# Three edits to a mixer-and-experts kernel: another order in the projection, another order of cells and mixers, and h2 computed in routing from x1

## The chip, the core and the metric

The kernel runs on one core of a Trainium2 chip. The core has TensorE (PE) for matmuls, VectorE (DVE), ScalarE (ACT) and GpSimd (POOL) for the rest, and SyncE (SP), which only issues transfers. The metric is the device time of one launch in microseconds (us); lower is better.

## The reference

One layer of a backbone for 1152 tokens of 1024 channels, all float32: 128 context tokens and 1024 latent ones.

```
h  = modulate(rmsnorm(x));  z = h @ w_in                      # 2832 columns
x  = x + gate1 * ([mLSTM(z) || windowed attention(z)] @ w_out)
h2 = modulate(rmsnorm(x, n2), sh2, sc2)
x  = x + gate2 * peer(h2)
def peer(h, ...):             # P_HEADS 8, P_DKEY 256, P_TOPK 16, N_KEYS 128
    q = h @ w_q                                       # 2048 columns
    sa, sb = q-halves against sub_a, sub_b            # 2 x 128 scores a head
    va, ia = top_k(sa, 16);  vb, ib = top_k(sb, 16)
    top, pos = top_k(va + vb, 16)                     # of 256 sums
    eidx = (ia * 128 + ib)[pos];  gates = softmax(top)
    a = gelu(h . u_tab[eidx]);  return sum((gates * a) * v_tab[eidx])
```

Each token picks 128 experts (8 heads, 16 each), and each expert is a row of u and a row of v, 8 KB together. The mLSTM runs over the tokens forward and backward; latent tokens start from cached states.

## The kernel before

The tokens are nine tiles of 128; tile 0 holds the context. Three stages follow one another.

*Conditioning* turns the conditioning vectors into shifts, scales and gates.

*Projection* (`project_in`, lines 280 to 560). A loop over the tiles, one body for each engine. TensorE turns the tile's normalised x (eight 128x128 blocks, `in_xn` to the PSUM banks `in_xT0` and `in_xT1`); VectorE and ScalarE copy the turned halves, scaled and shifted, to `in_hT`; TensorE multiplies by six column blocks of w_in (five of 512 columns, one of 272; b counts them), and other engines copy each block out, norm the attention heads, rotate them, and store all to DRAM. At the end of a tile q and k are turned, through the same two banks, and then the heads and the gates. `in_hT` exists once.

*Mixing and experts* (`mix_and_experts`). Four generators write each engine's program: `mlstm()` does 18 cell units of three steps each (two directions for each of nine tiles); `mixer(t)` does attention, w_out and x1 = x + gate1 * mix of a tile in 19 sub-steps and stores x1, h2 and h2 turned (h2T) to DRAM; `route(t)` loads h2T and does queries, scores, the top-16s and the expert numbers of a tile in 45 steps; `pair(t, r)` is the work on one pair of gathers. A tile's experts are 128 gathers in 64 pairs: a gather (line 992, GpSimd) brings one expert row for each of 128 partitions, 1.05 MB, into one of eight buffers `fx_ring`. Each of a pair's gathers serves 64 tokens with two slots each, so h2 lies in a buffer `fx_h2` with its 64 rows twice, and is loaded by four transfers of 64 partitions a tile. VectorE takes the dot product with h2 (line 1647), ScalarE the gelu and its weight, and TensorE adds the weighted v rows up (line 1239); then the buffer is free and GpSimd may issue the gather for the pair four further on. `route(t+1)` must have ended before the first gather of tile t+1.

The order is fixed by `drive`, the same on all engines. Ahead of the first gather (the lead) stand the cells, the mixer and the route of tile 0; the rest is interleaved with the pairs (the stream):

```
for _ in range(LEAD): next(cells)                                      # LEAD 4
for _ in range(SUBS): next(cells, None); next(subs)                    # SUBS 19
for _ in range(STEPS): next(cells, None); next(steps, None)            # STEPS 45
...
for r in range(PAIRS):
    pair(t, r)
    if t or r >= LAG: next(steps, None)                                # LAG 19
    if due(t, r): next(subs, None)
def due(t, r):
    return t == 0 and r < LAG or (t < 2 and r % 4 != 3) or t == 2
```

w_q is streamed in chunks of 0.52 MB, sixteen a tile, for the first `STREAMED` = 4 tiles, and then stays in SBUF as `rt_w_q`. SyncE issues the loads in program order: at the start of mixing the cached keys and values, masks, x, w_out, subT and wq, and behind them the cells' (`load_cell`). y of tile t-1 is stored in pair 12 of tile t.

## Time and profile before

| | before |
|---|---|
| median of 3 runs | 4085.48 us (4083.76 to 4090.05) |
| the profiled execution | 4090.53 us, of which the span 4088.7 us |
| mean granted clock of TensorE | 0.822 |
| PE, DVE, ACT, POOL busy | 69%, 58%, 24%, 35% of the span |
| gathers: share of 16 DMA engines' span | 72.2% |
| first and last gather issued | 915.8 us, 4065.4 us |

The busy shares are means over stages with different limits: ahead of the first gather the DMA queues are nearly empty, and behind it they are nearly full. Times in the trace count from the span's start. The projection's matmuls run from 119.68 to 576.21 us.

### The profile page before, as it was taken

To read this page: it belongs to the slowest core of one execution; us is meant where nothing else is said; L and a number is where in the kernel's file an instruction comes from. 1 tells how busy PE (TensorE), PEld (TensorE's weight loads), DVE (VectorE), ACT (ScalarE), POOL (GpSimd) and SP (SyncE) were. 2 spreads that over 40 slices of the span, in tenths; PEclk is the share of its full clock that TensorE was granted. 3 is DMA by queue.
4 is the path that set the end of the run, shared out by engine and by line. 5 is a ranking of instruction groups with operands and counts; after the bars stand their busy time and mean duration, and the time that the engine had idled before them with its cause. 6 is when DMAs were issued, how large, how long until landed. Compare 5 with 4: busy or idle time off the path is not lost.

```text
span 4088.7 us, 30827 instructions
## 1 busy us (share of the span) xinstructions
...
## 2 busy tenths in 40 slices
...
GB/s 411 54 42 42 42 116 94 169 120 404 401 404 351 416 405 384 420 420 404 371 420 405 411 421 406 421 409 403 421 407 403 421 410 421 405 401 421 421 422 371
DMA packets 228539, 1399.54 MB, mean 342 GB/s; under 512 B 25890, under 2 KB 36770, under 8 KB 75810
## 3 DMA queue, kind: packets, MB, share of 16 engines
q0 software_dynamic: 165888, 1208.03, 72.2%
q1 hardware_dynamic: 54724, 166.11, 11.0%
...
## 4 chain that ended last, share of the span: by engine, by line
DMA 43%; PE 19%; DVE 12%; issue 4%; POOL 4%; ACT 3%; SPq 0%; ACTq 0%; POOLq 0%; DVEq 0%
DMA fx_ring<-arg_uv,fx_eidx 40%; PE fx_acc L1239 10%; DVE fx_ring L1647 6%; POOL fx_ring L992 4%; PE at_sP L1107 2%; ACT fx_weighted_pick L1375 2%; DMA rt_wq<-arg_w_q 1%; PE rt_qP L1137 1%; DVE rt_rest L1527 1%; DVE rt_ab L1529 1%; DVE rt_rest L1525 1%; PE at_aP L1071 1%; DMA ml_v<-kv_scratch 1%; PE at_sP L1137 1%; ACT fx_gelu L1371 1%
## 5 line engine op out<-in xcount | busy, mean ns | idle before, releaser
L1239 PE MATMUL fx_acc<-fx_ring,fx_weighted_pick 128*64 128x512 f32 x4608 | 1495.1, 783 | 1046.6 <-ACT fx_weighted_pick L1375 1019.3
L1647 DVE CUSTOM_DVE_ANT_0 fx_ring<-fx_ring,fx_h 128x1024 f32<-128x1024 f32 x1152 | 1406.3, 1228 | 978.7 <-DMA fx_ring<-arg_uv,fx_eidx 973.7
L992 POOL DMA_INDIRECT fx_ring<-arg_uv,fx_eidx x1152 | 1318.3, 1144 | 1834.5 <-PE fx_acc L1239 1599.8
L1239 PEld LDWEIGHTS fx_acc<-fx_ring,fx_weighted_pick 128*64 128x64 f32 x4608 | 338.6, 164 | 2079.0 <-ACT fx_weighted_pick L1375 1488.8
L1371 ACT ACTIVATE fx_gelu<-fx_dot 128x2 f32<-128x2 f32 x576 | 117.1, 203 | 2287.1 <-DVE fx_dot L1647 2268.4
L411 PE MATMUL in_z<-w_in,in_hT 128*128 128x512 f32 (+1 forms) x864 | 365.7, 587 | 34.6 <-DVE in_hT L500 29.4
L1375 ACT ACTIVATE fx_weighted_pick<-fx_weighted_pick,fx_gelu 128x64 f32<-128x64 f32 x1152 | 338.1, 340 | 54.5 <-ACT fx_gelu L1371 1.5
L411 PEld LDWEIGHTS in_z<-w_in,in_hT 128*128 128x128 f32 x864 | 171.4, 200 | 224.9 <-issue 217.2
L1137 PE MATMUL rt_qP<-rt_w_q,rt_h2T 128*128 128x512 f32 x320 | 162.2, 630 | 0.0
L379 POOL COPY in_turned<-in_heads 128x320 f32<-128x320 f32 x9 | 4.1, 452 | 411.6 <-DVE in_heads L521 411.6
L1107 PE MATMUL at_sP<-at_w_out,at_mixT 128*128 128x512 f32 x288 | 133.8, 607 | 0.0
L1137 PE MATMUL rt_qP<-rt_wq,rt_h2T 128*128 128x512 f32 x192 | 106.5, 681 | 28.9 <-DMA rt_wq<-arg_w_q 22.3
L1018 POOL TENSOR_TENSOR ml_k<-ml_k,ml_cols 128x512 f32<-128x512 f32 x18 | 19.0, 1055 | 254.6 <-ACT ml_cols L1343 177.7
L249 DVE SCALAR_TENSOR_TENSOR gate_softplus<-gate_forget,gate_softplus 64x128 f32<-64x128 f32 x9 | 2.5, 283 | 178.4 <-ACT gate_softplus L242 178.4
L1639 DVE TENSOR_TENSOR fx_weighted_pick<-fx_pick,fx_gates 128x512 f32<-128x512 f32 x144 | 101.2, 703 | 2.1
L1647 DVE DVE_READ_ACCUMULATOR2_ANT fx_dot<- 128x1 f32 x1152 | 95.0, 82 | 0.0
L1137 PEld LDWEIGHTS rt_qP<-rt_w_q,rt_h2T 128*128 128x128 f32 x320 | 56.1, 196 | 113.8 <-issue 113.8
L1393 DVE CUSTOM_DVE_ANT_0 at_s<-at_sP,at_mask,at_sink_negated 128x512 f32<-128x512 f32 x72 | 52.5, 749 | 52.3 <-PE at_sP L1055 47.9
L1107 PEld LDWEIGHTS at_sP<-at_w_out,at_mixT 128*128 128x128 f32 x288 | 53.5, 194 | 77.3 <-issue 77.3
L1071 PE MATMUL at_aP<-att_v,at_pT 128*128 128x64 f32 x432 | 65.8, 293 | 0.0
L169 PE MATMUL ada_acc<-ada_w,ada_silu 128*2 128x512 f32 x192 | 41.2, 952 | 32.8 <-DMA ada_w<-arg_w_ada 32.8
L1055 PE MATMUL at_sP<-att_kT,at_qT 64*128 64x384 f32 x144 | 62.2, 514 | 0.0
(272 smaller groups left out, 2492.4 us busy)
## 6 DMA issues: line engine op xcount, KB each, us to landing
...
fx_ring<-arg_uv,fx_eidx POOLq DMA_INDIRECT x1152
...
fx_h<-h_scratch SPq DMA_DIRECT2D x36, 256.0 KB, 11.0
...
```

Source lines behind the costliest of these rows:

```text
L411: mm = pe.matmul(zp[b % 3][:, 0:n], hT[:, k, :], g.w_in[:, k, c0:c0 + n], start=(k == 0), stop=(k == KD - 1))
L992: pool.indirect_dma_start(out=ring[j][:], out_offset=None, in_=io.uv, in_offset=bass.IndirectOffsetOnAxis(ap=eidx[t % 2][:, i:i + 1], axis=0),
L1055: pe.matmul(ST[h % 2][:, P:4 * P], lhs, g.akT[half, t * P:t * P + 3 * P], start=True, stop=True).then_inc(s_sc, 1)
L1071: mm = pe.matmul(aP[:, h * ADH:(h + 1) * ADH], pT[h % 2][:, j * P:(j + 1) * P], rhs, start=(j == 0), stop=(j == 3))
L1107: mm = pe.matmul(ST[half][:], mixT[:, j, :], w_out[:, j, half * 512:(half + 1) * 512], start=(j == 0), stop=(j == KD - 1))
L1137: mm = pe.matmul(qq[b][:], hq2T[:, k, :], w[:, b * 512:(b + 1) * 512], start=(k == 0), stop=(k == KD - 1))
L1239: mm = pe.matmul(acc[b][cg * TOKS:(cg + 1) * TOKS, :], wsel[:, i % (2 * FILL), :], ring[i % GROUP][:, D + b * 512:D + (b + 1) * 512], star ...
L1371: act.activation(gelu[:, sl], dot[:, sl], ACT.Gelu_apprx_tanh).then_inc(s_gelu, 1)
L1375: last = act.activation(wsel[:, i, :], wsel[:, i, :], ACT.Copy, scale=gelu[:, i:i + 1])
L1393: dve.tensor_tensor_reduce(out=s[h % 2][:], in0=ST[h % 2][:], in1=mask[:], scale=-float(ADH) ** -0.5, scalar=nsink[:, h:h + 1], op0=ALU.ad ...
L1639: dve.tensor_tensor(wsel[:, lo:lo + FILL, :], pick[:].unsqueeze(1).to_broadcast([P, FILL, TOKS]), gates[t % 2][:, r * NC:r * NC + FILL].un ...
L1647: dve.tensor_tensor_reduce(out=ring[j][:, 0:D], in0=ring[j][:, 0:D], in1=h2r[t % 2][cg][:], scale=1.0, scalar=0.0, op0=ALU.mult, op1=ALU.a ...
```

## The change

1. *Projection.* `in_hT` exists twice. The turn of the next tile's x stands behind this tile's block 2 (`turn_x`), that of q behind block 4, and q and k are turned through a bank of their own, `in_qkTp`. ScalarE and VectorE scale the next tile's halves in between, GpSimd norms a tile ahead, and the loops are unrolled by two.
2. *Order in mixing.* The loads of the first two cells go to the head of SyncE's queue. Six cell steps stand ahead of the mixer (before: four), one beside every second sub-step of the mixer and of the first routing steps. A mixer has 15 sub-steps and a route 49. In the stream mixers take one sub-step in every pair of tiles 0 and 1; the route of tile 1 begins at pair 15 and takes five steps in four pairs. w_q is streamed for three tiles.
3. *h2 and h2T.* They are no longer stored or loaded. `route(t)` loads x1 (into the lower half of `rt_scores`, `x1r`), norms and turns it (k = 1 to 4), and at k = 28 and 29 makes the doubled rows of h2 with TensorE (`rows`), whose two halves VectorE and ScalarE copy to `fx_h2`.

```diff
-        hT = sb("in_hT", [P, KD, P])
+        hT = [sb(f"in_hT{i}", [P, KD, P]) for i in range(2)]
...
+        qkTp = psum("in_qkTp")
...
+                def turn_x(t):
                     pe.wait_ge(s_xn, t + 1)
-                    if not first:
-                        pe.wait_ge(s_qkTe, t * 2)
                     for k in range(KD):
                         mm = pe.transpose(xTp[k // 4][:, (k % 4) * P:(k % 4 + 1) * P], xn[:, k * P:(k + 1) * P], g.ident[:])
                     mm.then_inc(s_xT, 1)
+
+                def turn_head(t, i):
+                    pe.wait_ge(s_za, t * 4 + (i + 1))
+                    for h in range(MH):
+                        src = q[:, h * P:(h + 1) * P] if i == 0 else kv[:, h * P:(h + 1) * P]
+                        mm = pe.transpose(qkTp[:, h * P:(h + 1) * P], src, g.ident[:])
+                    mm.then_inc(s_qkT, 1)
+
+                def tile(t, par, first=False, last=False):
...
-                            mm = pe.matmul(zp[b % 3][:, 0:n], hT[:, k, :], g.w_in[:, k, c0:c0 + n],
+                            mm = pe.matmul(zp[b % 3][:, 0:n], hT[par][:, k, :], g.w_in[:, k, c0:c0 + n],
                                            start=(k == 0), stop=(k == KD - 1))
                         mm.then_inc(s_z, 1)
-                    for i in range(2):
-                        pe.wait_ge(s_za, t * 4 + (i + 1))
-                        for h in range(MH):
-                            src = q[:, h * P:(h + 1) * P] if i == 0 else kv[:, h * P:(h + 1) * P]
-                            mm = pe.transpose(xTp[i][:, h * P:(h + 1) * P], src, g.ident[:])
-                        mm.then_inc(s_qkT, 1)
+                        if b == 2 and not last:
+                            turn_x(t + 1)
+                        if b == 4:
+                            if not first:
+                                pe.wait_ge(s_qkTe, t * 2)
+                            turn_head(t, 0)
+                    pe.wait_ge(s_qkTe, t * 2 + 1)
+                    turn_head(t, 1)
...
+                    if not last:
+                        scaled(t + 1, 1 - par, 1)
...
-    SUBS = 19
+    SUBS = 15
...
-    LEAD = 4
+    LEAD = 6
     NG = NSIDE // 4
-    STEPS = 45
+    TURN = 4
+    ROWS = TURN + 24
+    STEPS = TURN + 45
     WQ = 2
-    STREAMED = 4
-    LAG = 19
+    STREAMED = 3
+    LAG = SUBS
...
     def due(t, r):
-        return t == 0 and r < LAG or (t < 2 and r % 4 != 3) or t == 2
+        return t < 2
 
     def drive(begin, pair, mixer, route, mlstm):
 
@@ -587,12 +628,14 @@
         for _ in range(LEAD):
             next(cells)
         subs = chain.from_iterable(mixer(t) for t in range(TILES))
-        for _ in range(SUBS):
-            next(cells, None)
+        for k in range(SUBS):
+            if k % 2:
+                next(cells)
             next(subs)
         steps = route(0)
-        for _ in range(STEPS):
-            next(cells, None)
+        for k in range(STEPS):
+            if k % 2 or k > 10:
                 next(cells, None)
...
                 if t or r >= LAG:
                     next(steps, None)
+                    if t == 0 and r % 4 == 3:
+                        next(steps, None)
...
+        x1r = sc[:, 0:NSIDE // 2, :].rearrange("p s k -> p (s k)")
...
-                        if k == 17:
-                            sp.wait_ge(s_hTe, t * 2 + 2)
-                            sp.dma_start(g.h2T_dram[t], h2T[:].rearrange("p k n -> p (k n)")).then_inc(s_hTo, 16)
-                            if t + 1 < TILES:
-                                sp.wait_ge(s_x1o, t * 16 + 16)
-                                sp.wait_ge(s_xn, t + 1)
-                                sp.dma_start(x1[:], io.x[t + 1]).then_inc(s_x, 16)
-                        if k == 18:
-                            sp.wait_ge(s_h2a, t + 1)
-                            sp.wait_ge(s_h2d, t + 1)
-                            sp.dma_start(g.h2_dram[t], h2[:]).then_inc(s_h2o, 16)
...
-                    if t:
-                        sp.wait_ge(s_qd, t * NSIDE)
-                    sp.wait_ge(s_hTo, t * 16 + 16)
-                    sp.dma_start(hq2T[:].rearrange("p k n -> p (k n)"), g.h2T_dram[t]).then_inc(s_hT, 16)
-                    for k in range(NSIDE):
-                        chunk(t * NSIDE + k + WQ)
-                        yield
-
-                def load_h2(t):
-                    sp.wait_ge(s_h2o, t * 16 + 16)
-                    if t >= 2:
-                        sp.wait_ge(s_dot, (t - 1) * SLOTS)
-                        sp.wait_ge(s_st, (t - 1) * 16)
-                    for cg in range(NC):
-                        for half in range(NC):
-                            sp.dma_start(h2r[t % 2][cg][half * TOKS:(half + 1) * TOKS, :],
-                                         g.h2_dram[t, cg * TOKS:(cg + 1) * TOKS, :]).then_inc(s_h[t % 2], 16)
+                    for k in range(STEPS):
+                        if k == 0 and t:
+                            sp.wait_ge(s_route, t)
+                            sp.wait_ge(s_x1o, t * 16 + 16)
+                            sp.dma_start(x1r, g.x1_dram[t]).then_inc(s_xr, 16)
+                        half, j = divmod(k - TURN, 11)
+                        if 0 <= half < 2 and j < KD:
+                            chunk(t * NSIDE + half * KD + j + WQ)
+                        yield
...
                 def begin():
-                    sp.wait_ge(s_hd, UNITS)
                     for d in range(2):
                         sp.wait_ge(s_hst[d], 16 * TILES)
-                    load_h2(0)
...
-                    if t == STREAMED - 2 and r == PAIRS - 12:
+                    if t == STREAMED - 2 and r == PAIRS - 4:
...
+                load_cell(0)
+                load_cell(1)
                 for cg in range(AKV):
...
+                    def turn_x1():
+                        pe.wait_ge(s_xn, t + 1)
+                        if t:
+                            pe.wait_ge(s_h2a, t * NC)
+                            pe.wait_ge(s_h2d, t * NC)
+                        for j in range(KD):
+                            mm = pe.transpose(qq[j // 4][:, (j % 4) * P:(j % 4 + 1) * P], qs[:, j * P:(j + 1) * P], g.ident[:])
+                        mm.then_inc(s_xT, 1)
+
+                    def rows(cg):
+                        pe.wait_ge(s_qT, t * NG + NG)
+                        if cg:
+                            pe.wait_ge(s_h2a, t * NC + cg)
+                            pe.wait_ge(s_h2d, t * NC + cg)
+                        for j in range(KD):
+                            for half in range(NC):
+                                mm = pe.matmul(qq[j // 4][half * TOKS:(half + 1) * TOKS, (j % 4) * P:(j % 4 + 1) * P],
+                                               hq2T[:, j, cg * TOKS:(cg + 1) * TOKS], g.ident[:], start=True, stop=True)
+                        mm.then_inc(s_h2p, 1)
+
                     for k in range(STEPS):
-                        half, j = divmod(k, 11)
-                        if half < 2:
+                        if k == 3:
+                            turn_x1()
+                        half, j = divmod(k - TURN, 11)
+                        if 0 <= half < 2:
                             if j < KD:
                                 query(half, j)
                             if j == 8:
@@ -1164,6 +1199,8 @@
                                 score(2 * half)
                             if j == 10:
                                 score(2 * half + 1)
+                        if ROWS <= k < ROWS + NC:
+                            rows(k - ROWS)
...
+                        if k == 1:
+                            if t:
+                                act.wait_ge(s_xr, t * 16)
+                            else:
+                                act.wait_ge(s_x1, 2)
+                            act.activation(qs, x1t, ACT.Square, accum_out=ss[:]).then_inc(s_sq, 1)
+                        if k == 2:
+                            act.wait_ge(s_ms, t + 1)
+                            act.activation(ss[:], ss[:], ACT.Sqrt).then_inc(s_rt, 1)
+                        if k == 3:
+                            act.wait_ge(s_rr, t + 1)
+                            act.activation(qs, x1t, ACT.Copy, scale=ss[:]).then_inc(s_xn, 1)
+                        if k == 4:
+                            act.wait_ge(s_xT, t + 1)
+                            cnd = min(t, 1)
+                            for j in range(4, KD):
+                                last = act.activation(hq2T[:, j, :], qq[1][:, (j - 4) * P:(j - 3) * P], ACT.Identity,
+                                                      bias=g.shift[:, 1, j, cnd:cnd + 1], scale=g.scale[:, 1, j, cnd:cnd + 1])
+                            last.then_inc(s_hTe, 1)
+                        if ROWS < k <= ROWS + NC:
+                            cg = k - ROWS - 1
+                            act.wait_ge(s_h2p, t * NC + cg + 1)
+                            if t >= 2:
+                                act.wait_ge(s_st, (t - 1) * 16)
+                            act.activation(h2r[t % 2][cg][:, 512:D], qq[1][:], ACT.Copy).then_inc(s_h2a, 1)
...
+                        if ROWS < k <= ROWS + NC:
+                            cg = k - ROWS - 1
+                            dve.wait_ge(s_h2p, t * NC + cg + 1)
+                            if t >= 2:
+                                dve.wait_ge(s_st, (t - 1) * 16)
+                            dve.tensor_copy(h2r[t % 2][cg][:, 0:512], qq[0][:]).then_inc(s_h2d, 1)
```

On TensorE's queue a tile of the projection stood like this (tile 0 before; `in_z` is a block's product, `in_xT` the turned x, and then q and kv):

```order
L395 MATMUL in_xT<-ident,in_xn 128x128 x8
L411 MATMUL in_z<-w_in,in_hT 128x512 x8
L411 MATMUL in_z<-w_in,in_hT 128x272 x8
L411 MATMUL in_z<-w_in,in_hT 128x512 x32
L418 MATMUL in_xT<-ident,in_q 128x128 x4
L418 MATMUL in_xT<-ident,in_kv 128x128 x4
L425 MATMUL in_aqTp<-ident,in_heads 128x128 x4
L426 MATMUL in_akTp<-ident,in_heads 128x128
L427 MATMUL in_akTp<-ident,in_gates 128x128
```

and now (tile 1 of the kernel after):

```order
L432 MATMUL in_z<-w_in,in_hT 128x512 x8
L432 MATMUL in_z<-w_in,in_hT 128x272 x8
L432 MATMUL in_z<-w_in,in_hT 128x512 x8
L408 MATMUL in_xT<-ident,in_xn 128x128 x8
L432 MATMUL in_z<-w_in,in_hT 128x512 x16
L415 MATMUL in_qkTp<-ident,in_q 128x128 x4
L432 MATMUL in_z<-w_in,in_hT 128x512 x8
L415 MATMUL in_qkTp<-ident,in_kv 128x128 x4
L448 MATMUL in_aqTp<-ident,in_heads 128x128 x4
L449 MATMUL in_akTp<-ident,in_heads 128x128
L450 MATMUL in_akTp<-ident,in_gates 128x128
```

The turn of x stands behind the third block and is the next tile's; that of q stands ahead of the last block.

On VectorE's queue, the last steps of the lead, the expert numbers of tile 0 (`rt_rest`, `rt_ab`) and the gates, before:

```order
L1527 TENSOR_TENSOR rt_rest<-rt_rest,rt_val 128x1024
L1529 TENSOR_REDUCE rt_ab<-rt_rest 128x64
L1525 TENSOR_TENSOR rt_rest<-rt_pos_partf,rt_iota 128x1024
L1527 TENSOR_TENSOR rt_rest<-rt_rest,rt_val 128x1024
L1529 TENSOR_REDUCE rt_ab<-rt_rest 128x64
L1525 TENSOR_TENSOR rt_rest<-rt_pos_partf,rt_iota 128x1024
L1527 TENSOR_TENSOR rt_rest<-rt_rest,rt_val 128x1024
L1529 TENSOR_REDUCE rt_ab<-rt_rest 128x64
L1535 SCALAR_TENSOR_TENSOR fx_eidx<-rt_ab 64x64 x4
L1538 TENSOR_REDUCE rt_gsum<-rt_gexp 128x8
L1539 RECIPROCAL rt_gsum<-rt_gsum 128x8
L1545 TENSOR_TENSOR fx_gates<-rt_gexp,rt_gsum 64x64 x4
```

and now, from the second of the four one-hot groups on, with cells (`ml_` names) between them:

```order
L1575 TENSOR_TENSOR rt_rest<-rt_pos_partf,rt_iota 128x1024
L1577 TENSOR_TENSOR rt_rest<-rt_rest,rt_val 128x1024
L1579 TENSOR_REDUCE rt_ab<-rt_rest 128x64
L1619 TENSOR_TENSOR ml_e<-fx_acc,ml_e 128x512
L1575 TENSOR_TENSOR rt_rest<-rt_pos_partf,rt_iota 128x1024
L1577 TENSOR_TENSOR rt_rest<-rt_rest,rt_val 128x1024
L1579 TENSOR_REDUCE rt_ab<-rt_rest 128x64
L1629 SCALAR_TENSOR_TENSOR ml_c<-ml_c,ml_cols,rt_qP 128x129 x2
L1634 TENSOR_TENSOR ml_num<-ml_num,fx_acc 128x258
L1629 SCALAR_TENSOR_TENSOR ml_c<-ml_c,ml_cols,rt_qP 128x129 x2
L1634 TENSOR_TENSOR ml_num<-ml_num,fx_acc 128x258
L1636 SCALAR_TENSOR_TENSOR ml_den<-ml_num 128x4
```

The last cell unit has moved from ahead of all of these rows into them.

On SyncE's queue, a late tile of the stream before (h2T for the next route, x1 and y of the tile before, h2 for the next tile):

```order
L863 DMA rt_h2T<-h2T_scratch 128x1024
L881 DMA fx_h_1_0<-x_scratch 128x1024
L885 DMA result_y<-fx_h_1_0 128x1024
L875 DMA fx_h_1_0<-h_scratch 64x1024 x2
L875 DMA fx_h_1_1<-h_scratch 64x1024 x2
L863 DMA rt_h2T<-h2T_scratch 128x1024
```

and now, two tiles (x1 for the next route, x1 and y of the tile before):

```order
L899 DMA rt_scores<-x_scratch 128x1024
L908 DMA fx_h_0_0<-x_scratch 128x1024
L912 DMA result_y<-fx_h_0_0 128x1024
L899 DMA rt_scores<-x_scratch 128x1024
L908 DMA fx_h_1_0<-x_scratch 128x1024
L912 DMA result_y<-fx_h_1_0 128x1024
```

The four loads of 64 partitions and that of h2T are gone, and one of x1 has come.

## Rows read from the trace of the kernel before

**Rows 1.** The page, DMA queues: packets, MB, share of 16 engines.

```profile
q0 software_dynamic: 165888, 1208.03, 72.2%
```

**Rows 2.** Line 992: count, issue ns (low, median, maximum), first to last start.

```profile
L992 POOL DMA_INDIRECT fx_ring<-arg_uv,fx_eidx x1152: 935/941/3041, 915.8 to 4065.4; - x192
```

**Rows 3.** Stretches: length; PE, PEld, DVE, ACT, POOL busy; PEclk, DMA share, GB/s.

```profile
3800.00:4000.00 200.00, 114.35 (x320) 24.96 (x318) 105.34 (x172) 31.58 (x120) 85.33 (x80) 0.75 1.01 422
2473.00:2805.00 332.00, 206.86 (x626) 54.60 (x628) 223.15 (x496) 59.16 (x208) 146.35 (x128) 0.81 1.01 413
1415.00:1789.00 374.00, 289.16 (x1096) 118.96 (x1096) 260.24 (x587) 132.34 (x324) 167.63 (x139) 0.89 1.00 406
1280.00:1320.00 40.00, 25.61 (x73) 8.00 (x73) 32.18 (x50) 6.28 (x19) 10.83 (x10) 0.82 0.61 245
2480.00:2500.00 20.00, 10.46 (x36) 3.85 (x35) 8.40 (x24) 3.17 (x11) 7.36 (x6) 0.83 1.02 341
850.00:915.00 65.00, 23.88 (x158) 20.26 (x156) 59.21 (x195) 9.68 (x36) 3.61 (x5) 0.70 0.28 85
```

**Rows 4.** GpSimd's timeline at the end of tile 0: start, length, row.

```profile
1306.79 0.94 POOL L992 DMA_INDIRECT fx_ring<-arg_uv,fx_eidx  x1 [20.60 <-PE fx_acc L1239]
```

**Rows 5.** Stretches of the projection, columns as in rows 3.

```profile
366.10:419.20 53.10, 44.79 (x119) 22.40 (x118) 15.20 (x34) 13.01 (x20) 2.70 (x3) 0.87 0.11 41
378.00:384.00 6.00, 5.92 (x7) 2.50 (x8) 0.00 (x0) 0.30 (x1) 0.00 (x0) 0.50 0.00 0
```

**Rows 6.** TensorE's timeline in the projection.

```profile
119.68 40.79 PE L411 MATMUL in_z<-w_in,in_hT 128*128 128x512 f32 x96 [1.69 <-ACT in_hT L440]
...
372.12 1.97 PE L395 MATMUL in_xT<-ident,in_xn 128*128 128x128 f32 x8 [4.32 <-ACT in_qkT L464]
378.08 41.31 PE L411 MATMUL in_z<-w_in,in_hT 128*128 128x512 f32 x96 [3.99 <-DVE in_hT L500]
...
576.21 0.60 PE L418 MATMUL in_xT<-ident,in_q 128*128 128x128 f32 x4
```

**Rows 7.** ScalarE's timeline in the projection.

```profile
412.56 0.60 ACT L453 ACTIVATE in_kv<-in_z 128x512 f32<-128x512 f32 x1 [6.27 <-PE in_z L411]
```

**Rows 8.** VectorE's timeline, the last cell step.

```profile
879.60 0.69 DVE L1591 TENSOR_TENSOR ml_h<-ml_num,ml_den 128x512 f32<-128x512 f32 x1
```

**Rows 9.** SyncE's queue at the start of mixing.

```profile
586.94 1.20 SPq L945 DMA_DIRECT2D at_cache_kT<-arg_cache_kT  x2
...
718.89 0.33 SPq L835 DMA_DIRECT2D x_scratch<-at_x  x1
```

**Rows 10.** VectorE's timeline at the start of mixing.

```profile
608.10 0.17 DVE L1658 TENSOR_SCALAR at_sink_negated<-at_sink 128x8 f32<-128x8 f32 x1 [20.83 <-DMA rt_subT<-arg_subT]
...
616.98 0.69 DVE L1569 TENSOR_TENSOR ml_e<-fx_acc,ml_e 128x512 f32<-128x512 f32 x1 [8.71 <-PE fx_acc L1209]
```

**Rows 11.** TensorE's timeline, the first query.

```profile
744.59 1.98 PE L1137 MATMUL at_sP<-rt_wq,rt_h2T 128*128 128x512 f32 x4 [2.05 <-DMA rt_h2T<-h2T_scratch]
```

**Rows 12.** VectorE by line, 600 to 877 us: busy, mean ns, idle before.

```profile
L1579 DVE SCALAR_TENSOR_TENSOR ml_c<-ml_c,ml_cols,rt_qP 128x129 f32<-128x129 f32 x68 | 20.5, 344 | 13.7 <-PE rt_qP L1218 13.6
L1584 DVE TENSOR_TENSOR ml_num<-ml_num,fx_acc 128x258 f32<-128x258 f32 x34 | 14.2, 417 | 1.0 <-PE fx_acc L1225 1.0
L1569 DVE TENSOR_TENSOR ml_e<-fx_acc,ml_e 128x512 f32<-128x512 f32 x18 | 12.5, 692 | 82.2 <-PE fx_acc L1209 76.1 <-issue 6.0
L1591 DVE TENSOR_TENSOR ml_h<-ml_num,ml_den 128x512 f32<-128x512 f32 x17 | 12.3, 725 | 0.6
```

**Rows 13.** VectorE by line, 2473 to 2805 us.

```profile
L1647 DVE CUSTOM_DVE_ANT_0 fx_ring<-fx_ring,fx_h 128x1024 f32<-128x1024 f32 x128 | 156.2, 1225 | 107.8 <-DMA fx_ring<-arg_uv,fx_eidx 107.1
L1639 DVE TENSOR_TENSOR fx_weighted_pick<-fx_pick,fx_gates 128x512 f32<-128x512 f32 x16 | 11.0, 690 | 0.3
L1647 DVE DVE_READ_ACCUMULATOR2_ANT fx_dot<- 128x1 f32 x128 | 10.6, 83 | 0.0
L1527 DVE TENSOR_TENSOR rt_rest<-rt_rest,rt_val 128x1024 f32<-128x1024 f32 x4 | 4.9, 1226 | 0.1
```

252 lines of the change are left out of this document (120 added, 132 removed).

## The prediction

> **What bounds the kernel now.** I read the page's queues first: the gathers of expert rows move 1208 MB [rows 1]. The first is issued at 915.8 us, the last at 4065.4 us [rows 2], so the kernel is a lead of 916 us and a stream of 4088.7 - 915.8 = 3173 us. Then the table of stretches. Where nothing runs beside the gathers, DMA is at a share of 1.01 and 422 GB/s, and VectorE is busy for half the time [rows 3]; 1208/422 = 2863 us, and the stream's other 310 us are other bytes and dips. Two kinds of dip stand in [rows 3]: 245 GB/s at a share of 0.61 for 40 us at the end of tile 0, and 341 GB/s *at a share of 1.02*, where the queues are full but slow. The first is a real gap: GpSimd, which issues the gathers, sat 20.60 us [rows 4]. The row names TensorE's last release, but the next gathers also need the route of the next tile, whose 45 steps begin at pair 19 and end exactly with pair 63. The stretches 1415 to 1789 and 2473 to 2805 are tiles from one store of y to the next, one with a mixer and one without: 374 and 332 us [rows 3], against 134.2/0.422 = 318 us for a tile's gathers alone.
>
> In the lead TensorE is the bound. A tile of the projection lasts 53.1 us and gives VectorE 15.20 and ScalarE 13.01 us of work [rows 5]. TensorE waits 4.32 us for a copy out of xT, turns xn, waits 3.99 us for hT, and needs 41.31 us for the six blocks [rows 6]; ScalarE sees a full block every 6.27 + 0.60 = 6.87 us [rows 7]. Behind the wait the granted clock is 0.50, the 1.2 GHz level [rows 5]. At the lead's end, from the last cell step at 879.6 us [rows 8], VectorE works alone until the first gather.
>
> **The change, part by part. Projection.** turn_x of the next tile moves behind block 2 of this one, hT gets a second buffer, q and k turn into a bank of their own. Five full blocks and the narrow one of 272 columns (6.87 x 272/512 = 3.65) are 38.0 us; eight turns of xn 1.0 (1.97 us at 1.2 GHz [rows 6], half of it at 2.4 GHz), q and k 1.0 for the same eight turns, heads and gates 0.6: 40.6 us a tile. The old waits are hidden by the blocks behind block 2 (some 20 us, against the 8.3 us of both waits). MATMULs now run from 119.68 to 576.21 us, 456.5 us [rows 6]. New: the first tile 41.31 + 1.5, as it still starts cold, and eight of 40.6, 367.6. **-89 us**; bounds -71 (the low clock returns at each seam, 41.31 - 38.0 = 3.3 us a tile, for part of the eight: 18 us) and -95. The work on the gates that stood behind the last tile now runs inside it, so the 10.7 us from 576.21 to the next stage's first issue at 586.94 [rows 6, 9] shrink by about 4: **-4**.
>
> **Cell loads.** They go ahead of 14 other loads. But VectorE's first operation waits for subT, the load behind w_out (608.10 [rows 10]), which now has the cells' bytes ahead of it. The first cell's VectorE step, 616.98 [rows 10], moves to about 611: -6 us, part of the walk below.
>
> **Lead-in steps.** Counted from the stage's start at 586.9, before: x1 stored at 132, first query 157.7 [rows 9, 11], gates 328 (first gather less 0.9). A cell unit, three steps, costs VectorE 20.5 + 14.2 + 12.5 + 12.3 us over 17 units, 3.5, with its small steps 4.0 [rows 12]. TensorE's share of one is 23.88/4 = 6.0 us, as four units fill its work between 850 and 915 [rows 3]; so a unit costs 4.0 to 10 us, a step 3.3 at most. Ahead of x1 stood 4 + 17 cell steps, now 6 + 7: eight fewer, 26 us. x1 comes at 132 - 6 - 26 = 100 if the mixer's own chain allows it and at 126 if it does not; I take 113. From there the norm, the turn and hT are five hops between engines; before they had a store and a load of h2T among them and took 25.7 us [rows 9, 11], I take 13: query at 126. From the query to 850 us, where the last scores are made (263 on this count), it took 105 us with 23 cell steps; now it is 19: 92, scores at 218. Now the bill for the cells put off: 20 steps stand behind the scores and not 8, four units more. The old remainder is the 65 us from 850 to 915, 59.21 of them VectorE's and 23.88 TensorE's [rows 3]. So 218 + 65 + 16 to 40. TensorE has 41 free us there, so I take 20 near the low end, and 3 for the copies of h2: 306. **-22 us**; bounds -1 and -40 (x1 at 100 and full overlap). The new row matmuls, 32 of 128 columns, lie between cell steps that wait for VectorE: nothing here, 8 us without that cover (four times 1.97 [rows 6]).
>
> **Stream, bytes.** One x1-sized tensor is 0.524 MB. Gone: h2 and h2T stores of 8 tiles 8.4 MB, h2T loads 4.2, h2 loads (both halves twice) 8.4, 16 chunks of w_q, as tile 3 reads the resident copy, 8.4. Added: 8 loads of x1, 4.2. Net -25.2 MB at 422 GB/s, **-60 us**. It counts in full because the share is 1.0 with a mixer or without [rows 3].
>
> **Stream, the slow load.** The dip to 341 GB/s is where the four h2 loads of 64 partitions run: (422 - 341) x 20 us = 1.6 MB, 3.8 us beyond their own bytes, eight times **-31 us** [rows 3]. The Trainium skill (SBUF — State Buffer, "Door 1: The DMA port swizzle") says that 64 partitions reach only half of the 16 ports, some 218 GB/s; by that the 1.05 MB would cost 4.8 instead of 2.5 us, eight times 18 us in all. The trace agrees in kind, and the sum goes by the row.
>
> **Stream, dips.** The route of tile 1 now takes five steps in four pairs from pair 15 and ends near pair 53, so the gap of [rows 4] goes: 40 us x (422 - 245)/422 = 17 us saved. Against it, mixers run a sub-step in *every* pair of tiles 0 and 1. Of VectorE's 223.15 us in a tile without a mixer, 156.2 + 10.6 + 11.0 are the gathers' dots and picks [rows 3, 13], 2.8 us a pair; the other 45 us are routing and y, in 34 of 64 pairs 1.3 us each. Mixer steps cost (260.24 - 223.15)/51 = 0.7, in the 51 of that stretch's pairs that have one. Together 4.8 us, against 5.9 us that a pair of tile 0 takes. Where a one-hot step runs (3 x 1.22 [rows 13]), a pair needs 7.2, for four pairs. I add 9 us in tile 0, 16 in tile 1 (16 more pairs with a mixer, and 8 us of new seams) and take off 8 in tile 2, free of mixers. Net 0; bounds -15 and +40. The norm chain in routing adds about 7 us of VectorE and ScalarE a tile in steps of up to 2 us, shorter than the eight buffers' lead. The x1 load for route(1) waits for a store only one step old, and ScalarE's Square behind it, with four pairs of gathers in flight. SyncE's wait on s_route ahead of x1r holds back nothing, as the old tile's y and x1 are issued by then.
>
> **Sum.** -89 - 4 - 22 - 60 - 31 + 0 = -206 us against the profiled execution's 4090.5 us, 3884; that one lies 5 us above the median of 4085.5, so 3879, of which I name 3878 us.
>
> **Rivals.**
> *A. The bytes were hidden (the stream is bound by the ring's round trip).* For it: GpSimd waits for TensorE's release of a buffer before a gather [rows 4]. Against: 422 GB/s at full share in the last tile. Then only lead and slow load gain: 3878 + 60 = 3938. 8 in 100.
> *B. Crowded tiles 0 and 1 cost more.* If each of the 120 pairs with a mixer step misses its time by 0.5 us: 3938 too. For it: 32.18 us of VectorE in the 40 us of 245 GB/s [rows 3]. 12 in 100. **The slower end:** the same place, if VectorE and TensorE run in turn: 260.24 + 289.16 = 549 us for a tile that takes 374 [rows 3], 175 more, two tiles 350: 4228. It decides from 104 us a tile on (207/2), 1.6 us a pair. Against: both overlap today. 2 in 100. The Trainium skill (SBUF — State Buffer, "Who interferes with whom") says that VectorE can block GpSimd's descriptor writing through their shared port; the trace shows a gather's issue at 0.941 us as median and 3.041 at most [rows 2], two of the latter a pair would be this case's mechanism.
> *C. The projection is not freed* (the chain of ScalarE's copies and table loads becomes its bound at 46 us a tile; only 13.01 us of work speak against): +43, 3921. 8 in 100.
> *D. More overlap:* lead -40, dips -15: 3845. 15 in 100.
> *E. Forecast as summed,* 55 in 100.
>
> **How the numbers follow.** The predicted time is E's. D and E's low side end near 3840; A, B and C lie at 3921 to 3938. The range 3838 to 3925 leaves out A, B and the slower end, 2 in 10. A difference of 0.2%, 8 us, is about what a measurement of this kernel can tell from none. All cases but the slower end are faster: 0.97, 0.01, 0.02.
>
> **What would show it.** Projection: MATMULs of one tile 40 to 41 us apart, clock 1.0, their end near 487. First gather near 800 us; VectorE's last ml_h within 7 us of the gates. No 341 GB/s at full share anywhere. No 20 us wait of GpSimd at tile 0's end, but dips near pairs 45 to 53. Period of late tiles 325 to 328 us. Wrong if the share falls below 0.9 for long in tiles 0 and 1, or if a tile of the projection takes over 44 us.

## The result and the profile after

The changed kernel took 3929.9 us (median of 4, 3924.5 to 3942.4) against 4086.6 us before; the ratio is 0.962 (95% interval 0.9596 to 0.9645). The prediction was 3878 us, with 3838 to 3925 as its range: the sign was right, the gain of 157 us was 52 us short, and the time lies outside the range. All times are medians of undisturbed runs: one run of `extra_late` of 9031 us, at a granted clock of 0.525, is left out.

Where the gain came from follows from four points of the trace. In the projection a tile lasts 40.4 us (before 53.1 [rows 5]), as TensorE's timeline shows between two turns of x:

```profile
380.92 1.04 PE L408 MATMUL in_xT<-ident,in_xn 128*128 128x128 f32 x8
381.80 13.90 PE L432 MATMUL in_z<-w_in,in_hT 128*128 128x512 f32 x32
...
421.33 1.04 PE L408 MATMUL in_xT<-ident,in_xn 128*128 128x128 f32 x8
```

421.33 - 380.92 = 40.4 us, no wait is noted, and the turn of eight blocks takes 1.04 us and not 1.97 [rows 6]. The last turn of kv stands at 482.8 us. SyncE's first issue of the next stage comes at 489.65, and the first gather at 804.7:

```profile
489.65 0.34 SPq L925 DMA_DIRECT2D ml_qkT<-qkT_scratch  x1
...
L1011 POOL DMA_INDIRECT fx_ring<-arg_uv,fx_eidx x1152: 935/941/3054, 804.7 to 3906.7; - x192
```

(SyncE's queue; then line 1011 as in [rows 2].) So the first gather comes 111 us earlier, where the working of the prediction has 115. The rest of the kernel is the stream: 3930.6 - 804.7 = 3125.9 us against 3172.9, 47 us less, where 91 were forecast. **44 of the 48 us that the profiled execution is off are in the stream.** Between stores of y its tiles took (us from the first gather or the last store):

| | to y of tile 0 | tile 1 | tile 2 | tiles 3 to 7, each |
|---|---|---|---|---|
| before | 499.1 | 373.8 | 352.6 | 331.6 to 333.2 |
| after | **516.8** | 367.5 | 325.2 | 326.1 to 327.2 |

The table of stretches says the same, with columns as in [rows 3]. To y of tile 0 before:

```profile
915.80:1415.00 499.20, 380.35 (x1454) 161.22 (x1455) 310.74 (x712) 177.76 (x423) 209.03 (x180) 0.87 0.97 392
```

After, to y of tile 0, then of tile 1, then a late tile:

```profile
804.70:1321.50 516.80, 422.90 (x1682) 195.28 (x1684) 314.68 (x707) 194.54 (x448) 214.09 (x180) 0.87 0.93 366
1321.50:1689.00 367.50, 287.85 (x1146) 122.14 (x1144) 248.52 (x568) 126.50 (x311) 158.55 (x132) 0.85 0.98 395
2340.70:2666.80 326.10, 209.01 (x698) 60.35 (x696) 225.72 (x503) 66.60 (x219) 144.71 (x128) 0.83 1.01 416
```

Late tiles run at full DMA share, 6.1 us shorter than before (the means of the five are 332.6 and 326.4 us). Tile 0 is longer than before although it moves fewer bytes, 366 GB/s x 516.8 us = 189 MB against 392 x 499.2 = 196; its share is 0.93 and was 0.97. GpSimd's 20.6 us wait of [rows 4] is gone. Before, it stood beside two others of over 9 us (10.95 and 9.25); now there are seven of 8.7 to 14.3 us up to y of tile 0. Two of them, with GpSimd's first columns as in [rows 4]:

```profile
917.54 1.19 POOL L1011 DMA_INDIRECT fx_ring<-arg_uv,fx_eidx  x1 [14.30 <-PE fx_acc L1276]
...
947.97 1.74 POOL L1011 DMA_INDIRECT fx_ring<-arg_uv,fx_eidx  x1 [12.23 <-PE fx_acc L1276]
```

**The first** has its cause on ScalarE's and SyncE's timelines. SyncE issued the load of x1 for routing at 903.07, and ScalarE, whose Square needs it, stood until it had landed, 8.5 us later; the gelus of the gathers waited behind. SyncE's queue, then ScalarE:

```profile
903.07 0.33 SPq L899 DMA_DIRECT2D rt_scores<-x_scratch  x1
...
898.20 0.59 ACT L1416 ACTIVATE fx_weighted_pick<-fx_weighted_pick,fx_gelu 128x64 f32<-128x64 f32 x2
911.60 1.06 ACT L1321 ACTIVATE rt_scores<-rt_scores 128x1024 f32<-128x1024 f32 x1 [12.82 <-DMA rt_scores<-x_scratch]
```

**The second** is a chain through all engines. The timeline of all engines, 932 to 949 us (rows of other work are left out):

```profile
932.76 0.20 ACT L1412 ACTIVATE fx_gelu<-fx_dot 128x2 f32<-128x2 f32 x1 [0.67 <-DVE fx_dot L1698]
933.06 0.59 ACT L1416 ACTIVATE fx_weighted_pick<-fx_weighted_pick,fx_gelu 128x64 f32<-128x64 f32 x2
933.20 1.98 PE L1151 MATMUL rt_qP<-rt_wq,rt_h2T 128*128 128x512 f32 x4
...
938.53 3.64 PE L1151 MATMUL rt_qP<-rt_wq,rt_h2T 128*128 128x512 f32 x4 [3.34 <-DMA rt_wq<-arg_w_q]
...
944.99 0.75 DVE L1434 CUSTOM_DVE_ANT_0 at_s<-at_sP,at_mask,at_sink_negated 128x512 f32<-128x512 f32 x1 [12.27 <-PE at_sP L1074]
...
945.75 1.94 PE L1276 MATMUL fx_acc<-fx_ring,fx_weighted_pick 128*64 128x512 f32 x8
945.79 0.72 ACT L1295 ACTIVATE at_s<-at_s,at_negmax 128x512 f32<-128x512 f32 x1 [10.84 <-DVE at_negmax L1434]
```

A pair's weights are ready at 933.65. Its accumulation (L1276) starts at 945.75, 12.1 us later, because two query steps stand ahead of it on TensorE's queue (an extra step), the second waits 3.34 us for its chunk of w_q and then runs at 3.64 us in place of 1.98 (the granted clock from 938.5 to 942.2 us is 0.54), and the mixer's matmuls follow. VectorE, ScalarE and GpSimd all wait for that one queue, and none of them was short of time.

### The profile page after: what moved, and what is told of

It reads as the page before. It is cut to its first block, busy times and chain, and to the rows that moved or that the text cites. A ratio compares the mean times of both kernels' runs of the same rounds, so it can differ in the third digit from the quotient of the medians.

```text
span 3930.6 us, 31619 instructions
## 1 busy us (share of the span) xinstructions
PE 2791.8 (71%) x10020; PEld 1090.0 (28%) x10020; DVE 2367.0 (60%) x5341; ACT 952.1 (24%) x2673; POOL 1419.3 (36%) x1269
## 4 chain that ended last, share of the span: by engine, by line
DMA 39%; PE 22%; DVE 13%; ACT 4%; issue 4%; POOL 4%; SPq 0%; ACTq 0%; POOLq 0%; DVEq 0%
DMA fx_ring<-arg_uv,fx_eidx 37%; PE fx_acc L1276 11%; DVE fx_ring L1698 7%; POOL fx_ring L1011 4%; PE at_sP L1128 3%; ACT fx_weighted_pick L1416 2%; DMA rt_wq<-arg_w_q 2%; PE at_aP L1090 1%; PE rt_qP L1151 1%; DVE rt_rest L1577 1%; DVE rt_ab L1579 1%; DVE rt_rest L1575 1%; PE at_sP L1074 1%; PE at_sP L1151 1%; ACT fx_gelu L1412 1%
## 5 line engine op out<-in xcount | busy, mean ns | idle before, releaser
L1276 PE MATMUL fx_acc<-fx_ring,fx_weighted_pick 128*64 128x512 f32 x4608 | 1471.5, 772 | 986.8 <-ACT fx_weighted_pick L1416 962.5
L1276 PEld LDWEIGHTS fx_acc<-fx_ring,fx_weighted_pick 128*64 128x64 f32 x4608 | 333.6, 161 | 1999.4 <-ACT fx_weighted_pick L1416 1446.7
L432 PE MATMUL in_z<-w_in,in_hT 128*128 128x512 f32 (+1 forms) x864 | 348.1, 561 | 1.7 <-DVE in_hT L533 1.7
L432 PEld LDWEIGHTS in_z<-w_in,in_hT 128*128 128x128 f32 x864 | 162.8, 191 | 168.5 <-issue 160.8
L1151 PE MATMUL rt_qP<-rt_w_q,rt_h2T 128*128 128x512 f32 x384 | 194.2, 629 | 0.0
L1151 PEld LDWEIGHTS rt_qP<-rt_w_q,rt_h2T 128*128 128x128 f32 x384 | 66.8, 194 | 132.5 <-issue 132.5
L1698 DVE DVE_READ_ACCUMULATOR2_ANT fx_dot<- 128x1 f32 x1152 | 94.9, 82 | 0.0
L1151 PE MATMUL rt_qP<-rt_wq,rt_h2T 128*128 128x512 f32 x128 | 68.1, 659 | 14.4 <-DMA rt_wq<-arg_w_q 14.3
L1484 DVE TENSOR_TENSOR at_xn<-at_sP,at_gate 128x512 f32<-128x512 f32 x18 | 12.4, 691 | 97.5 <-PE at_sP L1128 97.5
```

Of the source, the lines that this page charges most:

```text
L432: mm = pe.matmul(zp[b % 3][:, 0:n], hT[par][:, k, :], g.w_in[:, k, c0:c0 + n], start=(k == 0), stop=(k == KD - 1))
L1151: mm = pe.matmul(qq[b][:], hq2T[:, k, :], w[:, b * 512:(b + 1) * 512], start=(k == 0), stop=(k == KD - 1))
L1276: mm = pe.matmul(acc[b][cg * TOKS:(cg + 1) * TOKS, :], wsel[:, i % (2 * FILL), :], ring[i % GROUP][:, D + b * 512:D + (b + 1) * 512], star ...
L1698: dve.tensor_tensor_reduce(out=ring[j][:, 0:D], in0=ring[j][:, 0:D], in1=h2r[t % 2][cg][:], scale=1.0, scalar=0.0, op0=ALU.mult, op1=ALU.a ...
```

## The experiments

All are variants of the changed kernel, except `p_only`. "Edit" shows what differs. To see where a kernel loses its time in tile 0, I read the issue times of the gathers off GpSimd's timeline. The figures are us between pairs, so 12 pairs at the gathers' own rate are 60 us:

| pairs | 0-14 | 14-26 | 26-44 | 44-60 | 60-64 | 0-64 |
|---|---|---|---|---|---|---|
| before | 71.6 | 70.7 | 113.9 | 94.1 | 40.6 | 391.0 |
| after | 69.6 | 85.8 | 140.5 | 99.6 | 21.9 | 417.3 |
| after_again | 68.4 | 84.9 | 132.6 | 104.7 | 21.9 | 412.4 |
| late_norm | 70.4 | 76.1 | 135.6 | 101.1 | 22.7 | 405.8 |
| extra_early | 71.3 | 84.4 | 130.4 | 95.5 | 24.3 | 405.9 |
| extra_late | 69.1 | 77.7 | 115.2 | 105.4 | 24.8 | 392.1 |
| no_extra | 68.3 | 76.8 | 115.0 | 93.1 | 41.8 | 394.9 |
| late_noextra | 72.2 | 65.3 | 110.2 | 96.5 | 48.3 | 392.5 |
| best1 | 69.4 | 65.3 | 113.3 | 94.9 | 30.5 | 373.3 |
| best2 | 111.6 | 75.0 | 106.2 | 94.3 | 32.2 | 419.1 |
| no_chunks | 71.5 | 81.2 | 116.7 | 99.6 | 23.4 | 392.4 |

### The projection alone

The kernel before with `project_in` of the changed one.

> The kernel before with the changed projection alone. The trace of the changed kernel has a projection tile every 40.4 us and MATMULs from 120 to 483 us (before: to 576 us), so if the projection's gain reaches the end undiminished the time is 4086.6 - 93 - 4 = 3990 us. If it were partly given back behind it (cell loads or tables that were hidden before), 4000 us or more.

3990.2 us (ratio 0.9758, 0.9742 to 0.9775), 95 us less than before. The projection's gain arrives whole.

### The extra routing steps and the norm chain

```diff
 no_extra:
-                    if t == 0 and r % 4 == 3:
-                        next(steps, None)
 late_norm (Square at k == 3, and all of the chain two later):
-    TURN = 4
+    TURN = 6
-                        if k == 1:
+                        if k == 3:
```

> The changed kernel without the extra routing step in tile 0 (one step a pair from pair 15, 49 steps, so the route of tile 1 ends exactly with pair 63 again). Theory 1 (tile 0 is crowded: a mixer step in every pair and five routing steps in four pairs queue behind each other on TensorE and ScalarE): less crowding in pairs 15 to 53, but the wait for the route at the end of tile 0 comes back, 15 to 20 us; sum 3920 to 3935 us. Rival (the loss is one stall of ScalarE for the x1 load, crowding costs nothing): the wait alone comes back, 3930 + 17 = 3947 us.

> The changed kernel with the norm, turn and copies of x1 two routing steps later (the Square at step 3, the load of x1 still at step 0), so that a load that is 8.5 us under way has three pairs, 18 us, to land. In the changed kernel ScalarE stood 12.8 us for that load in tile 0 and GpSimd 14.3 us behind it. Theory 2 (this stall is lost time for the ring): 10 to 14 us less, 3918 us. Theory 1 alone (the ring would have been late anyhow): 3928 to 3932 us.

no_extra took 3894.6 us (0.9539, 0.9523 to 0.9555): 35 us *less*, below all that either theory gave, although GpSimd stood 21.85 us for the route at tile 0's end again. late_norm took 3919.3 us (0.9588, 0.9572 to 0.9604), 10.6 less. That is no more than the spread of this kernel (see after_again below), so the pairs 14 to 26 of the table must carry the reading: there the stall is 9 to 10 us between the changed kernel and late_norm, and 11.5 us between no_extra's 76.8 and late_noextra's 65.3. The load's stall was lost time. late_norm did not remove it whole: beside the extra step of pair 15 the Square still came early, ScalarE stood 5.41 us for the load, and GpSimd 13.93 us behind it. In best1, which has no extra step there, ScalarE's wait is 1.81 us, and in late_noextra there is none.

### Which extra steps

```diff
 extra_early:
-                    if t == 0 and r % 4 == 3:
+                    if t == 0 and r % 4 == 3 and r < 36:
 extra_late:
+                    if t == 0 and r % 4 == 3 and r >= 36:
```

> The changed kernel with the extra routing steps of tile 0 only at pairs 15 to 35 (six of thirteen, all while routing does its queries and scores on TensorE with streamed chunks of w_q). Without any extra step the kernel took 3894.6 us, 35 us less than with thirteen, although a wait of 21.9 us for the route stood at tile 0's end again. Theory T (the extra steps cost where they put two query steps, their chunks and a mixer step behind one pair on TensorE): nearly all of the loss is here, 3920 to 3930 us. Theory V (they cost where VectorE's top-16 and one-hot steps pile up): none of it is here, and the route ends at pair 57, so 3880 to 3890 us.

> The changed kernel with the extra routing steps of tile 0 only at pairs 39 to 63 (seven of thirteen, behind the queries and scores). Theory T: the loss of the early steps and the wait for the route at tile 0's end are both gone, 3875 to 3888 us. Theory V: the loss is here, 3915 to 3930 us.

extra_early took 3907.6 us (0.9555, 0.9539 to 0.957), extra_late 3901.4 (0.9537, 0.9514 to 0.956). Neither theory holds by itself, though the early steps cost far more than the late ones. By the medians the groups cost 13 and 7 us net of the wait that they save. From the first gather to y of tile 0 it took 484.4 us in no_extra, 503.0 in extra_early, 489.3 in extra_late, and 516.8 and 511.4 in the two profiles with all thirteen steps. Up to pair 44 the early ones cost (71.3 + 84.4 + 130.4) - (68.3 + 76.8 + 115.0) = 26 us for six steps, 4.3 us a step, and save 15 us behind pair 44. The late ones cost 12 us between pairs 44 and 60 for four of them, and save 17 in the last four pairs. The last column flatters the steps: in no_extra, which has the wait, the 12 pairs behind it were issued and worked off in 89.5 us, in the changed kernel in 99.5, so about half of the saved wait is paid back there.

### Mixer steps spread, and the bytes

```diff
 streamed4, and old_due:
-    STREAMED = 3
+    STREAMED = 4
 old_due:
-        return t < 2
+        return t == 0 and r < LAG or (t < 2 and r % 4 != 3) or t == 2
```

> The changed kernel with the mixers' steps spread over tiles 0 to 2 as before (three pairs in four of tiles 0 and 1, the rest in tile 2) and w_q streamed for four tiles, as the resident copy needs the mixers' memory: 8.4 MB more, 20 us by the bytes. Theory 1 (a mixer step in every pair crowds tiles 0 and 1): 13 steps fewer in tile 0 and 8 in tile 1 give back a part of the 45 us that tile 0 lost, say 10 to 15: 3930 + 20 - 12 = 3938 us. Rival (bytes hidden behind a ring that is bound otherwise): 3918 us. Rival (crowding by mixers costs nothing): 3950 us.

> The changed kernel with w_q streamed for four tiles and not three, nothing else: 16 chunks of 0.524 MB more in tile 3, a tile at full DMA share. If bytes count in full, 8.4 MB at 421 GB/s are 20 us: 3950 us. If they are hidden (rival A of the prediction), 3930 us.

old_due took 3924.8 us (0.9607, 0.9591 to 0.9623), streamed4 3940.8 (0.9643, 0.9626 to 0.9661). By the medians the 8.4 MB cost 11 us. The two tiles that carry them (from y of tile 0 to y of tile 2) took 707.8 us and not 692.7, 15 us of the 20 that the bytes need at full rate; against after_again's 688.2 it is 19.6. So bytes count, wholly or nearly so. Beside streamed4, 21 mixer steps fewer in tiles 0 and 1 are worth 16 us.

### What TensorE waits for: work or chain

```diff
 less_query (queries of tile 1 at half width; half of them are left out):
-                            mm = pe.matmul(qq[b][:], hq2T[:, k, :], w[:, b * 512:(b + 1) * 512],
+                            n = 256 if t == 1 else 512
+                            mm = pe.matmul(qq[b][:, 0:n], hq2T[:, k, :], w[:, b * 512:b * 512 + n],
 no_chunks (no chunk is loaded or waited for in the route of tile 1; it is routed by other weights):
-                    if m < NSIDE * STREAMED:
+                    if m < NSIDE * STREAMED and not NSIDE <= m < 2 * NSIDE:
```

> The changed kernel with the query matmuls of tile 1's route (in tile 0 of the stream) at 256 columns and not 512, so that half of tile 1's queries are left out; everything else is issued as before. That takes 16 times 1 us of matmuls at 2.4 GHz off TensorE in the crowded pairs, and no byte and no wait. Theory P (TensorE's own work is what the ring waits for there, as the table of stretches has it at 20.0 of 20 us in several): 15 to 30 us less, 3900 to 3915 us. Theory C (it waits for chunks and for other engines' steps, and its work fits): within 6 us of 3930.

> The changed kernel without the 16 chunks of w_q for tile 1's route: its queries are made from the chunks left in the two buffers, so tile 1's experts are others, and no query matmul of that route waits for a load. 8.4 MB less. TensorE waited 13.6 us for chunks in tile 0. If these waits hold nothing, at most the bytes go: 0 to -20 us, 3910 to 3930. Theory C (a chunk wait holds the accumulate of the gathers behind it): bytes and waits together, -25 to -40 us, 3890 to 3905.

less_query took 3916.5 us (0.9587, 0.9568 to 0.9605), 13 us less for 16 us of matmuls taken away. no_chunks took 3902.9 (0.9543, 0.9527 to 0.9559), 27 us less, and tile 0's 64 pairs shrank by 24.9 us (20.0 against after_again's 412.4), where its 8.4 MB alone would be 20 us at full rate. The two runs don't settle the question. less_query's gain hints that TensorE's work counts, but it is hardly more than the spread of this kernel. no_chunks' gain can't be told from the price of its bytes, so that the chunk waits themselves cost something is seen in the timeline above and not shown by this run. best2 has neither queries nor chunks in the pairs where it loses time.

### Better orders of tile 0

```diff
 best1 (late_norm, and):
-                    if t == 0 and r % 4 == 3:
+                    if t == 0 and r % 4 == 3 and r >= 40:
 best2 (late_norm and no_extra, and):
-    LAG = SUBS
+    LAG = 8
-        return t < 2
+        return t == 0 or (t == 1 and r % 6 != 5)
+                if t == 0 and r < 7:
+                    next(subs, None)
 best4 (best1, and):
-        return t < 2
+        return t == 0 and r not in (47, 51, 55, 59) or (t == 1 and r < 60)
```

> Both repairs together: the norm chain two routing steps later, and extra routing steps in tile 0 only at pairs 43 to 63 (six, which make the 51 steps end at pair 59). Theory T with the stall of the x1 load taken away (measured alone at -10.6 us): 3868 to 3880 us. If the two gains are one and the same, 3880 to 3890 us. Theory V: 3905 us or more.

> The order of tile 0 built on what was measured: two mixer steps in each of the first seven pairs, where no routing runs and the ring ran at the gathers' own rate, the route of tile 1 from pair 8 on at one step a pair with no extra steps (its 51 steps end at pair 58), the norm chain two steps later, and one pair in six of tile 1 without a mixer step. best1 took 3883 us with tile 0's 64 pairs in 373 us. If the first pairs have room for two mixer steps and single routing steps fit beside a mixer step: 3865 to 3878 us. If the doubled mixer steps only move the crowd: 3883 to 3900 us.

> The changed kernel with the norm chain two steps later and no extra routing step: 51 steps from pair 15 on at one a pair, so two of them are left over and run at the end of tile 0, behind pair 63. Against no_extra (3894.6 us) the stall of 13.8 us for the x1 load goes, and two steps more stand behind the last pair. If the stall is worth what it was in late_norm: 3884 us. If the two left-over steps lengthen the wait at tile 0's end by their own time: 3890 us. Against best1 (3883.1), which has six extra steps late and no such wait.

> best1 with the mixer pausing in pairs 47, 51, 55 and 59 of tile 0, where two routing steps stand, and taking those four steps in tile 1 (every pair up to 59). If three steps in one pair are what still costs in pairs 44 to 60 of tile 0, 2 us each: 3873 to 3878 us. If those steps are hidden there, 3881 to 3886 us.

best1 took **3883.1 us** (0.9499, 0.9483 to 0.9515), 47 us less than the changed kernel and the best of all. In the same 206 us from pair 14 on, the changed kernel and best1 read:

```profile
874.00:1080.00 206.00, 169.90 (x640) 79.40 (x642) 101.01 (x255) 75.58 (x168) 69.56 (x60) 0.88 0.89 349
```

```profile
874.00:1080.00 206.00, 190.12 (x797) 87.15 (x797) 128.68 (x305) 84.85 (x197) 92.54 (x78) 0.98 1.01 417
```

The slower kernel (first) has TensorE *less* busy, 170 us against 190, at a lower granted clock (0.88 against 0.98), 60 GpSimd instructions done against 78, and 349 GB/s. So TensorE's sum of work was not the bound there.

best2 took 3909.7 us (0.9561, 0.9544 to 0.9577). It is the cleanest case of the mechanism: two mixer steps a pair in pairs 0 to 6, and nothing else beside the gathers. The first 14 pairs took 111.6 us and not best1's 69.4. The 42 us are those of the seven added steps, 6 us each: the seven intervals that wait for pairs 0 to 6 took 79.0 us and not 35.4. No engine was full; TensorE was busy for 84 of 112 us, at a granted clock of 0.69, and the others for under 43:

```profile
803.00:915.00 112.00, 84.21 (x284) 40.45 (x284) 42.14 (x82) 38.17 (x82) 36.37 (x33) 0.69 0.70 270
```

and its waits (who for whom: us in total, times, longest) go in a ring:

```profile
POOL fx_ring L1011 <- PE fx_acc L1276: 69.9, 10, 10.6
...
DVE at_s L1434 <- PE at_sP L1074: 37.7, 7, 10.3
ACT at_s L1295 <- DVE at_negmax L1434: 26.8, 7, 7.9
```

TensorE's scores, VectorE's maximum, ScalarE's exponential, and TensorE again: two such chains in one pair stand one behind the other in every queue. Behind pair 20 best2 ran as fast as best1, one step of each kind a pair.

late_noextra took 3899.5 us (0.9522, 0.9508 to 0.9537), 9 us more than its higher expectation: two steps left over at the end made GpSimd's wait for the gates 28.51 us. best4 took 3888.3 us (0.9505, 0.9492 to 0.9518), which can't be told from best1; the third step in those pairs costs nothing that I could find.

### The lead, and transfers of 64 partitions

```diff
 old_lead, and best3 on best1 (one cell step beside every step):
-    LEAD = 6
+    LEAD = 4
-            if k % 2:
-                next(cells)
+            next(cells)
-            if k % 2 or k > 10:
-                next(cells, None)
+            next(cells, None)
 halves_b (best1; the same for the load of x1 ahead of y):
-                            sp.dma_start(x1r, g.x1_dram[t]).then_inc(s_xr, 16)
+                            for hf in range(2):
+                                ps = slice(hf * 64, hf * 64 + 64)
+                                sp.dma_start(x1r[ps, :], g.x1_dram[t, ps, :]).then_inc(s_xr, 16)
```

old_loads is best1 with `load_cell(0)` and `load_cell(1)` back at the head of `mlstm()`; after_again is the changed kernel unaltered.

> The changed kernel with the lead's cells as before: four cell steps ahead, then one beside every sub-step of the mixer and every step of routing (cell loads and h2 stay as changed). The prediction gave the deferred cells 20 to 25 us of the lead. First gather then at 825 to 830 us and not 804.7, time 3950 to 3955 us. If it was the h2 round trip through DRAM that the lead gained from, and not the cells: first gather 805 to 812 us, 3930 to 3937 us.

> The changed kernel itself once more, beside the others. Its four runs went from 3924 to 3942 us, and a kernel with the same tile 0 (streamed4) had that tile in 497.8 us where the first profile had 516.8. If tile 0's length varies from run to run, this median is anywhere from 3915 to 3935 us and the tile differs from 516.8 by over 5 us. If it doesn't, 3930 us and 516.8 within 3 us, and old_lead's 13 us are due to its order of cells.

> best1 (3883.1 us, runs within 6 us of each other) with the lead's cells as in the kernel before: four cell steps ahead and one beside every step. If the order of cells does nothing to the lead (old_lead had its first gather 2 us earlier than the changed kernel), 3880 to 3886 us. If the changed order gains what the prediction gave it, 3895 us or more. If the old order gains, 3870 to 3878 us.

> best1 with the first two cells' loads back behind the fourteen others. The prediction had the first cell step on VectorE 6 us earlier by the move. If that 6 us is all and reaches the first gather: 3889 us. If it is swallowed by TensorE's work behind it: 3883 us. If the loads are where the lead's whole 14 us came from: 3895 us.

> best1 with both loads of x1 in the stream (for routing and for y, 16 of 0.524 MB) split into two transfers of 64 partitions each, issued one behind the other; same bytes. If transfers of 64 partitions run slow beside the gathers as the four h2 loads seemed to, the dip of 341 GB/s comes back: 3.8 us for 1.05 MB, so some 30 us in all, 3913 us. If the h2 loads were slow for another reason (each row of h2 was read twice), 3883 to 3887 us.

old_lead took 3916.8 us (0.9573, 0.9555 to 0.9592), with its first gather at 802.65 us, 2 us earlier than the changed kernel's. after_again took 3926.8 (0.9608, 0.9584 to 0.9632), and its way to y of tile 0 511.4 us and not 516.8: a crowded tile 0 isn't the same length in every execution, so single differences of some 10 us between kernels that have it (old_lead, streamed4, late_norm, less_query) can't be put down to their edits by the median alone. The lead scatters too: in nine profiles that share the changed kernel's lead the first gather came between 802.4 and 809.4 us, so old_lead's 2 us say only that the order of cells matters little. On the steadier best1, the old order of cells (best3) took 3887.2 us (0.9513, 0.9497 to 0.9529): the changed order gains 4 us, and the walk gives it 13 + 13 - 20 = 6 (x1 earlier, the way to the scores shorter, the bill behind them). old_loads took 3894.4 (0.9528, 0.9511 to 0.9545), 11 us more. Its first gather was 3.8 us later, which is within that scatter, and to y of tile 0 and of tile 1 it took 5.7 and 3.7 us more than best1. Why loads ahead of the first gather should act there, no run shows.

halves_b took 3910.3 us (0.9574, 0.9557 to 0.9591), 27 us more than best1 for the same bytes. The 20 us from the load of x1 on, in halves_b and then in best1:

```profile
2582.00:2602.00 20.00, 8.96 (x26) 2.14 (x28) 9.83 (x18) 3.16 (x12) 7.97 (x8) 0.82 1.02 381
```

```profile
2566.00:2586.00 20.00, 10.91 (x32) 2.61 (x32) 11.19 (x19) 3.16 (x12) 8.37 (x8) 0.75 1.02 422
```

(422 - 381) x 20 us are 0.8 MB, 1.9 us for one load of 0.524 MB, where [rows 3] gave 3.8 for two. A split also makes two small transfers of one; that the size isn't the cause shows in the kernel before, where three loads of 0.262 MB to all 128 partitions (`at_mix`, `at_h_square`, `at_sigmoid`) were issued from 1656.15 us on and the rate stayed whole:

```profile
1651.00:1671.00 20.00, 11.51 (x38) 3.55 (x36) 9.39 (x17) 5.65 (x15) 7.00 (x7) 0.74 1.02 422
```

The Trainium skill (SBUF — State Buffer, "Door 1: The DMA port swizzle") has 64 partitions reach half of the ports, some 218 GB/s. An estimate from that page's figure is that the 16 split loads (8.4 MB) cost 8.4/0.218 - 8.4/0.422 = 19 us more. The run says 27, and the run decides.

## Why the prediction was wrong

- **Projection, -89:** right. -93 to the last turn of kv in the trace, 95 in `p_only`. The tail's -4 is 3.9: 10.7 us before, 489.65 - 482.8 = 6.9 now.
- **Lead-in steps, -22:** too large. From the stage's first issue to the first gather it was 328.9 us and is 315.0, so -14 (309.9 to 318.1 us in the nine profiles with this lead). Counted from that issue, x1 is stored at 124 us where the walk took 113, the first query comes at 131 (126), the last scores start at 224 (218), and the first gather at 315 (307). So the eight cell steps fewer brought x1 forward by 8 us together with the moved loads, and not by 19; a part of that came back in the shorter way from x1 to the query. The bill behind the scores, 91 us, is close to the walk's 88. best3 prices the order at 4 us and old_loads the moved loads at 11.
- **Bytes, -60, and the slow load, -31:** right in kind. A late tile shrank from 332.6 to 326.4 us, 6.1 against the 6.4 of the two terms together. halves_b shows that the 64 partitions are the cause. Rival A, bytes hidden, is out: streamed4 paid for its chunks, by the intervals 15 to 20 of 20 us.
- **Dips, net 0: the step that failed.** To y of tile 0 the steps had some -17 for the wait and +9 for crowding, -16 for the 6.5 MB that tile 0 no longer moves and -4 for its slow load, some -27 in all; it came out 17.7 us longer than before. These 45 us are the whole miss of the stream. The prediction's own sign of being wrong, a share below 0.9 for long, came with them: 0.89 for the 206 us from pair 14 on. Most of the dips lay between the gathers of pairs 19 and 41 and not, as it had said, near 45 to 53. Two sentences of that step were wrong.
  1. "The x1 load for route(1) waits for a store only one step old, and ScalarE's Square behind it, with four pairs of gathers in flight" priced this at nothing. It was a 12.8 us stall of ScalarE and 14.3 us of GpSimd, worth some 9 to 11.5 us (pairs 14 to 26 of late_norm, no_extra and late_noextra): four pairs in flight don't cover a load of 8.5 us when the gelu of the next pair is behind it.
  2. The route "now takes five steps in four pairs", with "40 us x (422 - 245)/422 = 17 us saved". Not taking them is worth 35 us (no_extra). The step summed VectorE alone, 4.8 of 5.9 us, and never asked what a pair costs as a chain. A second step in a pair cost 6 us where no engine was full (mixer steps, best2) and 4.3 us beside queries and chunks (routing steps, extra_early).

With both mended the same edits give 3883.1 us (best1), 5 us from the 3878 forecast, and its tile 0 takes 468.2 us, 31 less than before, where the steps had 27. Part of that is luck, since the lead-in steps fell 8 us short and the projection gave 4 more than forecast.
- **Rival B** named the place and 3938 us, from VectorE as the engine that runs short. The place was right. The engine was not: it is the order of the queues, with TensorE's wait for chunks in it. B's own price, 0.5 us for each of 120 pairs, hides that the loss is lumpy. What I had against its stronger form, "both overlap today", holds for one step a pair only.
- **Rivals C and D** did not come about.

That the chance put on B was 12 in 100 is the lesson for the range: its own row, 32.18 us of VectorE in 40 us at 245 GB/s [rows 3], told of a dip with VectorE *not* full.
